# Where the operands of a matmul stream begin in SBUF: the eight tiles of a weight ring each 16 bytes further past a multiple of 512, and three activation tensors at 384, 128 and 256 bytes past one

## The reference, cut to what matters

```python
x = x + rmsnorm(concat(mla_attention * silu(gate), fox_attention * silu(gate)) @ w_out)   # first block
x = x + 0.5 * ((silu(n(x) @ w_gate) * (n(x) @ w_up)) @ w_down)      # ffn1, 2048 -> 5632 -> 2048
x = x + (sigmoid(g_att) * y_att + sigmoid(g_sg) * y_sg) @ w_out_2   # mixer: windowed attention, spatial gate
x = x + 0.5 * swiglu(n(x))                                          # ffn2
out = rmsnorm(x)
```

## Time and profile before

| | kernel before |
|---|---|
| median of the executions | 2704.9 us |
| profiled execution | 2706.09 us |
| its span, first to last instruction | 2704.3 us |
| mean granted TensorE clock | 0.997 of full speed |
| TensorE matmul (PE) | 2670.6 us busy, 99% |
| TensorE weight load (PEld) | 2209.5 us, 82% |
| VectorE (DVE) | 1431.3 us, 53% |
| ScalarE (ACT) | 1189.7 us, 44% |
| memory traffic | 183 GB/s over the span |

### The profile page before, as it was taken

How to read it: one execution, slowest core, us unless ns; L and a number is a source line. 1 busy time by engine, 2 the same in 40 slices (tenths; PEclk the granted TensorE clock), 3 DMA queues, 4 the chain that set the end, 5 groups by cost and what they waited for, 6 DMA issues and landing times.

```text
span 2704.3 us, 32516 instructions
## 1 busy us (share of the span) xinstructions
PE 2670.6 (99%) x12171; PEld 2209.5 (82%) x12171; DVE 1431.3 (53%) x1563; ACT 1189.7 (44%) x1362; POOL 26.7 (1%) x24
## 2 busy tenths in 40 slices
PE   8999999899999999999999999999999999999998
PEld 6888878788888888888888888888888888888886
DVE  6755555654555455555445655555654545554554
ACT  4544554444444444444444554444444444443333
POOL 0000000000000000000000300000000000000000
PEclk9999999999999999999999999999999999999999
DMA  6655545466666665667666445666566666666664
GB/s 195 205 150 155 165 139 187 140 196 190 190 188 191 187 191 188 191 192 231 192 193 190 152 141 178 190 191 193 182 207 188 189 189 187 193 187 191 193 192 148
DMA packets 258672, 496.23 MB, mean 183 GB/s; under 512 B 17602, under 2 KB 19992, under 8 KB 258328
## 3 DMA queue, kind: packets, MB, share of 16 engines
q1 hardware_dynamic: 257040, 489.81, 60.4%
q0 software_dynamic: 896, 4.89, 0.5%
q10 hardware_dynamic: 648, 0.32, 0.0%
HBM read 492.86 MB, written 2.10 MB: 183 GB/s over the span
## 4 chain that ended last, share of the span: by engine, by line
PE 98%; DVE 1%; DMA 0%; ACT 0%; issue 0%; ACTq 0%; DVEq 0%
PE acc L431 93%; PE tr L447 3%; PE s_ps L486 1%; PE o_ps L509 1%; DVE act_lo L1151 0%; DMA fix<-fixed 0%; PE tr L715 0%; DVE xres L1498 0%; ACT act_hi L806 0%; DVE stats L1171 0%; DVE wlo L1119 0%; DVE u L1674 0%; ACT lat L853 0%; DVE xres L1737 0%; DVE xres L1267 0%
## 5 line engine op out<-in xcount | busy, mean ns | idle before, releaser
L1119 DVE TENSOR_TENSOR wlo<-raw,whi 128x1024 fp32r<-128x1024 f32 x929 | 1135.7, 1225 | 1048.8 <-ACT whi L776 1024.8
L776 ACT ACTIVATE whi<-raw 128x1024 fp32r<-128x1024 f32 x929 | 978.9, 1057 | 1107.8 <-PE acc L431 1103.1
L431 PE MATMUL acc<-whi,act_hi 128*128 128x512 f32 (+1 forms) x2560 | 1008.6, 394 | 6.4 <-DVE wlo L1119 4.3
L431 PE MATMUL acc<-whi,act_lo 128*128 128x512 f32 (+1 forms) x2560 | 996.8, 389 | 0.0
L431 PE MATMUL acc<-wlo,act_hi 128*128 128x512 f32 (+1 forms) x2560 | 995.7, 389 | 0.0
L431 PEld LDWEIGHTS acc<-whi,act_hi 128*128 128x128 f32 x2560 | 481.8, 188 | 104.3 <-issue 5.3
L431 PEld LDWEIGHTS acc<-whi,act_lo 128*128 128x128 f32 x2560 | 481.4, 188 | 100.7
L431 PEld LDWEIGHTS acc<-wlo,act_hi 128*128 128x128 f32 x2560 | 482.2, 188 | 95.7
L431 PE MATMUL acc<-whi,h_hi 128*128 128x512 f32 x704 | 274.3, 390 | 0.0
L431 PE MATMUL acc<-whi,h_lo 128*128 128x512 f32 x704 | 274.0, 389 | 0.0
L431 PE MATMUL acc<-wlo,h_hi 128*128 128x512 f32 x704 | 273.9, 389 | 0.0
(11 more groups left out here) (211 smaller groups left out, 1305.4 us busy)
## 6 DMA issues: line engine op xcount, KB each, us to landing
raw<-in_w_in SPq DMA_DIRECT2D x280, 512.0 KB, 4.1
raw<-in_ffn_w_gate SPq DMA_DIRECT2D x176, 512.0 KB, 4.4
raw<-in_ffn_w_up SPq DMA_DIRECT2D x176, 512.0 KB, 4.2
raw<-in_ffn_w_down SPq DMA_DIRECT2D x176, 512.0 KB, 4.6
raw<-in_w_out SPq DMA_DIRECT2D x64, 512.0 KB, 4.2
raw<-in_w_sg_out SPq DMA_DIRECT2D x24, 512.0 KB, 4.6
raw<-in_w_uq SPq DMA_DIRECT2D x9, 512.0 KB, 4.1
raw<-in_w_ukv SPq DMA_DIRECT2D x8, 512.0 KB, 4.8
```

The lines of the kernel that those rows point to most:

```text
L431: last = nc.tensor.matmul(pair[:, half, 0:width], left[:, k, tok], right[:, slot, t, 0:width], start=(k == 0 and n == 0), stop=(j == count ...
L776: nc.scalar.activation(whi[:, slot, :, 0:width], raw[:, slot, :, 0:width], ACT.Copy).then_inc(hi_ready, 1)
L1119: nc.vector.tensor_tensor(wlo[:, slot, :, 0:width], raw[:, slot, :, 0:width], whi[:, slot, :, 0:width].bitcast(F32), ALU.subtract).then_in ...
```

## The change

Three things about where tensors begin, and nothing about what is computed or in which order:

- `LINE` is 512 instead of 2048, so that start, region and `q_at` are rounded to 512.
- `whi` and `wlo` get rows of `STEP` = 516 elements instead of 512, of which 512 are used. Tile n of the ring's eight begins at 2064 n bytes, which is 16 n past a multiple of 512: 0, 16, 32, ... 112 for `whi`. `whi` is now 16512 bytes long, so `wlo` begins 128 past a multiple and its tiles are at 128, 144, ... 240; `fix` (the identity matrix and masks) begins at 256.
- `o` begins at 384, `h` at 128 and `merged` at 256 past a multiple of 512; `g_sb`, `h_sb` and `gfinal`, which follow `h`, are at 128 too. `act`, `lat`, `sg` and `att` stay at multiples of 512, and so does `raw`.

The two tiles of a group no longer touch each other in `whi` and `wlo`, so the ACTIVATE at L776 and the TENSOR_TENSOR at L1119 have operands of 128x2x512 where they had 128x1024. The program of every engine has the same instructions in the same order.

```diff
-        LINE = 2048
+        LINE, STEP = 512, W + 4
...
         raw, top = place_at("raw", [P, RING, TILES, W], F32, top)
-        whi, top = place_at("whi", [P, RING, TILES, W], F32R, top)
-        wlo, top = place_at("wlo", [P, RING, TILES, W], F32R, top)
+        whi, top = place_at("whi", [P, RING, TILES, STEP], F32R, top)
+        wlo, top = place_at("wlo", [P, RING, TILES, STEP], F32R, top)
...
-        o_hi, top = place_at("o_hi", [P, KD, SEQ], F32R, q_at)
-        o_lo, top = place_at("o_lo", [P, KD, SEQ], F32R, top)
+        o_hi, top = place_at("o_hi", [P, KD, SEQ], F32R, q_at + 384)
+        o_lo, top = place_at("o_lo", [P, KD, SEQ], F32R, q_at + 384 + KD * SEQ * 4)
...
-        h_hi, top = place_at("h_hi", [P, KF, SEQ], F32R, region)
+        h_hi, top = place_at("h_hi", [P, KF, SEQ], F32R, region + 128)
...
-        merged_at = top
-        merged_hi, top = place_at("merged_hi", [P, KD, SEQ], F32R, top)
-        merged_lo, top = place_at("merged_lo", [P, KD, SEQ], F32R, top)
+        merged_at = region + 2 * SG_GROUPS * SEQ * 4
+        merged_hi, top = place_at("merged_hi", [P, KD, SEQ], F32R, merged_at + 256)
+        merged_lo, top = place_at("merged_lo", [P, KD, SEQ], F32R, merged_at + 256 + KD * SEQ * 4)
```

More of the change, by code:

```diff
@@ L217, in build @@
         sg_hi, top = place_at("sg_hi", [P, SG_GROUPS, SEQ], F32R, region)
-        sg_lo, top = place_at("sg_lo", [P, SG_GROUPS, SEQ], F32R, top)
-        merged_at = top
-        merged_hi, top = place_at("merged_hi", [P, KD, SEQ], F32R, top)
-        merged_lo, top = place_at("merged_lo", [P, KD, SEQ], F32R, top)
+        sg_lo, top = place_at("sg_lo", [P, SG_GROUPS, SEQ], F32R, region + SG_GROUPS * SEQ * 4)
+        merged_at = region + 2 * SG_GROUPS * SEQ * 4
+        merged_hi, top = place_at("merged_hi", [P, KD, SEQ], F32R, merged_at + 256)
+        merged_lo, top = place_at("merged_lo", [P, KD, SEQ], F32R, merged_at + 256 + KD * SEQ * 4)
         qk2, top = place_at("qk2", [P, HALVES, 2 * ATT_W], F32, region)
```

## The result

The changed kernel takes 2755.9 us (2755.66 and 2756.14) against 2704.9 (2704.71 and 2705.09): +51.0 us, a ratio of 1.0189 with a 95% interval of 1.0145 to 1.0232. It is slower, by 1.9%. The profiled execution has a span of 2753.9 us against 2704.3, at the same granted clock of 0.997.

A forecast was written before the change was run, and what follows sets the result against it. TensorE's distance between matmul starts was taken to bound the kernel. All terms were about 0, so 2706.1 + 0 = 2706.1 us profiled, 2705 as median; likeliest case 2699 to 2711, 8-in-10 range 2635 to 2790.

The forecast's parts named there:

- the cover: ScalarE and VectorE work three groups ahead of TensorE; over 1.5 us per group must be lost before PE notices.
- one number rules: L431 on TensorE: time between two matmul starts, 226.7 ns over 11,052 wide matmuls, 2505 of 2704 us.
- The broken form: Splits at L776 and L1119 with 128x2x512 operands: at most 10 ns each, no path cost except some 0.02 us at the start.
- R1: Every L431 matmul: changing starts lose the settled state, +4.4 ns a step, +49 us, 2754, up to 2808; chance 0.28.
- the likeliest case: The forecast itself: starts change nothing at the matmuls, all being a switching cost; 2699 to 2711 us, chance 0.41.
- the term for the starts: New starts of weight tiles, `o`, `h` and `merged` at the L431 matmuls: price taken as 0.
- two equal transpose jobs: Float32 jobs from `fox`, 64 bytes past a multiple, and `qk`, at one: both 0.60 us, weak evidence that starts cost nothing.
- Its bounds, -148 and +103: Matmul starts: all 13.4 ns vanish, 148 us off; or every step takes about 236 ns, +103 us.
- R2: L431 matmuls: equal starts clash, so shifted tiles run faster; 2566 us if all goes, about 2635 if half; chance 0.23.
- The 13.4 ns beyond the columns at full clock: L431 step of 226.7 ns against 213.3 for 512 columns, in sum 148 us; perhaps clashing reads or weight switching.
- R3: Matmul reads by 64 bytes: six of eight tile starts touch one unit more, 6.7 ns each, +55 us, 2760; chance 0.08.
- The two rules against the change: Skill's independent TensorE read ports and 16-byte SBUF cachelines: by either no new start matters, sum unchanged at 2705 us.

The follow-up runs named there:

- 0/64: Survey against the kernel before: weight tiles at multiples of 512, left operand `h` 64 bytes past one; 233.3 ns a step, whole kernel 2773.2 us.
- 0/16: Survey against the kernel before: weight tiles at multiples of 512, left operand `o` 16 bytes past one; 226.7 ns a step, whole kernel 2730.0 us.
- 0/32: Survey against the kernel before: weight tiles at multiples of 512, left operand `act` 32 bytes past one; 233.3 ns a step, whole kernel 2773.2 us.
- 32/16: Survey against the kernel before: weight ring 32 bytes past a multiple of 512, left operand `o` 16 past; 226.8 ns a step, whole kernel 2757.5 us.
- 128/16: Survey against the kernel before: weight ring 128 bytes past a multiple of 512, left operand `sg` 16 past; 226.7 ns a step, whole kernel 2748.6 us.
- 0/4: Survey against the kernel before: weight tiles at multiples of 512, left operand `att` 4 bytes past one; 232.2 ns a step, whole kernel 2730.0 us.

## Why the prediction was right and wrong

**Right: the place and the cover.** That one number rules, the step, at 11.05 us per nanosecond, holds: 51.0 us are 4.6 ns a step. The broken form was given at most 10 ns and no cost on the path; it is 1060 and 1229 ns here, and the kernel with 256 bytes of padding shows 0 in total. The range of 2635 to 2790 us holds too, but only because it took in R1; the likeliest case, 2699 to 2711, did not come.

**Wrong: the term for the starts, taken at 0.** The forecast of 2705 rested on "steady pieces over quite different tensors agree to 0.1 ns" and on two equal transpose jobs. The first compared only starts at equal distance 0 modulo 256, so it could not speak of any other; the second was a float32 job, and float32 transposes keep their 109 ns a pass in every kernel here, also where the float32r steps are slow. In place of 0 the term measured 4.6 ns x 11,052 = 51 us. Its bounds, -148 and +103, held. The better evidence was in the prediction already: steps that vary behind a transpose, and a cost that is there at the full clock alone. For the latter it called the clock of the earlier trace rows half; the profile records no granted clock before 18.1 us, so that was read from the steps, but a recorded 0.50 from 499.4 to 509.6 us of the kernel before, with steps of 426 or 427 ns, bears it out.

**R1: right in price, in sign and in what shows it, its cause not borne out.** It gave 2754 us from the unsettled steps behind a transpose (231.1 ns), and 44.4 and 233 us for the pieces; measured are 2755.9, 44.4 and 234.4. But it said that the relation of load and stream is lost because it changes at every tile. The ring at one start of 16 has no such change and costs as much, and `h` alone at 128 loses its 5.8 ns against tiles all at 0. So change from tile to tile is not needed for the loss. Whether it adds anything where it is there, in the changed kernel, no run separates; and since single pairs of starts range from 226.7 to 234.3 ns, the match of 231.1 with the measured 231.2 may be luck. That part of R1 which said that the relation hangs on address as well as on time stands: the 226.7 ns come back at distance 0 with M at 0, 32, 64 and 128, and one pair settles at 226.7 or 228.3.

**R2: no.** In none of over 40 pairs of starts does a settled mean go under 226.6 ns, while the changed kernel's single steps do (down to 224 ns), with longer ones beside them. The 13.4 ns beyond the columns at full clock were not removed by any start tried. Whether all of them come from reads that clash is open: no run took the weight loads away.

**R3: no.** It would leave multiples of 64 free; 0/64 costs 6.6 ns. Nor are there two cheap tiles in the changed kernel: over its matmuls on `act` the steps behind the eight ring tiles average 230.8 to 232.7 ns, and those behind tiles 0 and 4, which R3 would spare, 231.5 each.

**The two rules against the change.** The rows show up to 7.6 ns a step from nothing but starts. The Trainium skill, "TensorE: Matmul & The Clock Gate", Part 2, has the two read ports independent, so that a load takes no read bandwidth from a running matmul. The prediction drew from it that no address can matter, and that did not come true: at the full clock most pairs of different starts cost 2 to 7.6 ns. That the load takes bandwidth is not shown by this; the runs show only that the step depends on where the two begin. The Trainium skill, "SBUF — State Buffer", note on cachelines under Door 1, has cachelines of 16 bytes. By these every start of the change would be free, and it was not; that a left start of 4 or 8 costs and 0/16 does not would fit, but 0/32 at 233.3 ns does not. Why the period is 256 bytes is not settled by these runs.

## What to carry to other kernels

In a dense stream of float32r matmuls, each with its own weight load, begin stationary and moving tiles at the same place modulo 256 bytes, and the moving ones at a multiple of 32 (0, 32, 64 and 128 were tried). Of the other pairs most cost 1 to 3.4% of the step here and a few (0/16, 32/16, 128/16) next to nothing. Pad tiles by 256 bytes or not at all; 16 bytes of padding alone lost 45 of the 51 us. Where the trace has all operands at one kind of start, its evenness says nothing about another kind; the varying steps just behind an interruption were the better hint.

## What the runs showed of the hardware that was not expected

- Steps settle on a few values. 226.7, 228.3, 229.0, 230.0, 231.1, 231.7, 232.4 and 233.3 ns come back over tensors and kernels; 233.3 - 226.7 is 6.7 ns, 16 periods of the 2.4 GHz clock.
- Which of them a piece takes can differ for equal addresses, but in a regular order. Within each feed-forward stage, the last piece aside, the pieces of `act` take turns between 44.17 and 44.80 us with everything at 16, between 43.55 and 43.85 us with `act` at 240 and the ring at 0, and run 44.38, 44.38, 44.17 us with ring and `act` at 48. What sets the order is open.
- With `wlo` at 128 the executions spread from 2758.6 to 2768.6 us (the kernel before beside them: 2704.8 to 2706.5). That they settle differently from one execution to the next is not shown; the kernel with everything at 16, which has two levels too, spreads by 0.5 us only.
- At a granted clock of 0.50 no start cost anything: 426 or 427 ns a step in all fourteen kernels.
- A start 4 bytes off counts: 0/4 has 232.2 ns.
- One moved operand of three spoils the others' steps too: with `wlo` alone at 128, the steps behind `whi` past `act_hi` average 234.6 ns and those behind `whi` past `act_lo` 230.7, though both pairs begin at distance 0; behind `wlo` past `act_hi`, the one with distance 128, it is 233.0.
